# Order of the PSUM banks in the down projections, and the split of the convolution's taps and the turning of the residual in the odd stage

## The reference, cut to what matters

```python
def swiglu(h, w_gu, w_down):
    g, u = jnp.split(h @ w_gu, 2, axis=-1)
    return (jax.nn.silu(g) * u) @ w_down

def _odd_mixer(h, w_in, conv_w, conv_b, ln_g, ln_b, w_out):
    proj = jnp.einsum('bsd,de->bse', h, w_in)
    val, gt, z = three slices of CONV_CHANNELS each
    g = (val * jax.nn.sigmoid(gt)).astype(jnp.float32)
    c = lax.conv_general_dilated(g, kern, window_strides=(1,), padding=[(CONV_KERNEL - 1, 0)],
        dimension_numbers=('NWC', 'WIO', 'NWC'), feature_group_count=CONV_CHANNELS)   # 31 taps a channel
    c = c + conv_b
    mu, var = mean and variance of c over the channels
    c = (c - mu) * lax.rsqrt(var + LN_EPS) * ln_g + ln_b
    y = jax.nn.silu(c) * jax.nn.silu(z)
    return jnp.einsum('bse,ed->bsd', y, w_out)
...
x = x + _odd_mixer(rmsnorm(x), ...)
return _rmsnorm(x, final_norm)
```

## Time and profile before

| what | value |
|---|---|
| time, median of 3 runs | 1538.62 us (1537.76 to 1538.62) |
| span of the profiled execution | 1539.7 us, 1.1 above that median |
| PE busy | 1481.8 us, 96% of the span |
| DVE, ACT, POOL busy | 886.2, 619.4, 381.8 us |
| mean granted clock of TensorE | 0.988 of full speed |
| DMA | 178.45 MB, 116 GB/s over the span |

### The profile page before, as it was taken

How to read it: one execution, slowest core, us unless ns; L and a number is a source line. 1 busy time by engine, 2 the same in 40 slices (tenths; PEclk the granted TensorE clock), 3 DMA queues, 4 the chain that set the end, 5 groups by cost and what they waited for, 6 DMA issues and landing times. The chain is left out here.

```text
span 1539.7 us, 19037 instructions
## 1 busy us (share of the span) xinstructions
PE 1481.8 (96%) x7030; PEld 1168.6 (76%) x7030; DVE 886.2 (58%) x1265; ACT 619.4 (40%) x943; POOL 381.8 (25%) x493
## 2 busy tenths in 40 slices
PE   5999999999999999899999999999999999999998
PEld 3788888888877777458888888888777778777656
DVE  5767425633573566846633434422556556798986
ACT  3432212222443443745542222222531235777755
POOL 3111001000000000013003888520202100599930
PEclk9899999999999999999999999999999999999999
DMA  9887625333244122003433333373124223222211
GB/s 347 279 279 260 203 83 181 107 109 101 59 119 116 55 69 73 8 15 89 130 89 109 123 110 96 112 265 96 55 82 126 81 86 116 75 70 77 75 55 55
DMA packets 203878, 178.45 MB, mean 116 GB/s; under 512 B 7451, under 2 KB 182095, under 8 KB 203286
## 3 DMA queue, kind: packets, MB, share of 16 engines
q1 hardware_dynamic: 187462, 121.87, 26.8%
q0 software_dynamic: 15184, 53.41, 9.9%
q10 hardware_dynamic: 1152, 2.10, 0.4%
HBM read 168.89 MB, written 8.46 MB: 115 GB/s over the span
## 5 line engine op out<-in xcount | busy, mean ns | idle before, releaser
L2053 PE MATMUL ps<-h_hi,w_hi 128*128 128x512 f32 x1176 | 473.4, 403 | 2.7 <-DVE us L1800 1.2
L2055 PE MATMUL ps<-h_hi,w_lo 128*128 128x512 f32 x1176 | 459.0, 390 | 0.0
L2054 PE MATMUL ps<-h_lo,w_hi 128*128 128x512 f32 x1176 | 458.7, 390 | 0.0
L1280 DVE TENSOR_TENSOR w_lo<-w_stage,w_hi 128x1024 fp32r<-128x1024 f32 x225 | 292.1, 1311 | 219.4 <-ACT w_hi L802 216.9
L802 ACT ACTIVATE w_hi<-w_stage 128x1024 fp32r<-128x1024 f32 x225 | 230.8, 1048 | 186.5 <-PE ps L2055 166.8
L2053 PEld LDWEIGHTS ps<-h_hi,w_hi 128*128 128x128 f32 x1176 | 221.2, 188 | 64.4 <-issue 17.2
L2054 PEld LDWEIGHTS ps<-h_lo,w_hi 128*128 128x128 f32 x1176 | 221.4, 188 | 48.7 <-issue 5.0
L2055 PEld LDWEIGHTS ps<-h_hi,w_lo 128*128 128x128 f32 x1176 | 221.0, 188 | 47.1
L2053 PE MATMUL ps<-a_hi,w_hi 128*128 128x512 f32 x480 | 188.3, 392 | 3.7 <-issue 1.8
L2054 PE MATMUL ps<-a_lo,w_hi 128*128 128x512 f32 x480 | 187.4, 390 | 0.0
L2055 PE MATMUL ps<-a_hi,w_lo 128*128 128x512 f32 x480 | 187.3, 390 | 0.0
(11 more groups left out here) (456 smaller groups left out, 1697.8 us busy)
## 6 DMA issues: line engine op xcount, KB each, us to landing
w_stage<-in_w_gu SPq DMA_DIRECT2D x88, 512.0 KB, 4.2
ada_w<-in_w_ada POOLq DMA_DIRECT2D x72, 512.0 KB, 6.3
w_stage<-in_w_down SPq DMA_DIRECT2D x44, 512.0 KB, 3.6
w_stage<-in_w_in SPq DMA_DIRECT2D x24, 512.0 KB, 3.8
w_stage<-in_odd_w_in SPq DMA_DIRECT2D x24, 512.0 KB, 3.7
w_stage<-in_even_w_in SPq DMA_DIRECT2D x16, 512.0 KB, 3.8
w_stage<-in_w_out SPq DMA_DIRECT2D x8, 512.0 KB, 3.7
mats<-mats_d POOLq DMA_DIRECT2D x4, 1024.0 KB, 6.8
```

The costliest lines, as they stand in the source:

```text
L1280: dve.tensor_tensor(w_lo[:, c % RING], w_in[:, c % RING], w_hi[:, c % RING].bitcast(F32), ALU.subtract).then_inc(w_split, 1)
L2053: pe.matmul(bank, w_hi[:, slot, k], rhs_hi, start=start, stop=False, skip_group_check=True)
L2054: pe.matmul(bank, w_hi[:, slot, k], rhs_lo, start=False, stop=False, skip_group_check=True)
L2055: return pe.matmul(bank, w_lo[:, slot, k], rhs_hi, start=False, stop=stop, skip_group_check=True)
```

## The change

It has three parts.

1. In each of the four down projections the step j = 0 goes through the banks in the order 4, 5, 6, 2, 3, 0, 1, 7. The waits are set apart: none of the three is ahead of banks 4 to 6; bank 2 waits for the product of hidden tile 9, bank 0 for that of tile 10, bank 7 (in the first layer) for `mod_ready`. The steps j = 1 to 10 are as they were.
2. In the odd stage POOL takes 12 taps of each of the first six tiles, and DVE 18. The last two tiles are as they were.
3. The residual is turned in two banks: tiles 1, 3 and 5 in bank 6, the others in bank 7; two tiles at a time after n = 2, 4 and 6, tile 6 after n = 8, tile 7 after n = 10. ACT copies them in the step after. The first sum into bank 6 at n = 8 waits for six copies.

```diff
+DOWN_FIRST = [4, 5, 6, 2, 3, 0, 1, 7]
...
-POOL_TAPS = [13] * 6 + [10, 7]
+POOL_TAPS = [12] * 6 + [10, 7]
 DVE_TAPS = [TAPS - 1 - p - q for p, q in zip(POOL_TAPS, PE_TAPS)]
...
+TURNED_AT = {2: [0, 1], 4: [2, 3], 6: [4, 5], 8: [6], 10: [7]}
+TURN_IN_6 = (1, 3, 5)
+
+
+def turn_bank(kt):
+
+    return 6 if kt in TURN_IN_6 else 7
...
-                    if 4 <= n < 4 + KT:
-                        act.wait_ge(x_turned, n - 3)
-                        act.activation(xT[:, n - 4], ps[7][:], ACT.Copy).then_inc(x_back, 1)
+                    for kt in TURNED_AT.get(n - 1, ()):
+                        act.wait_ge(x_turned, kt + 1)
+                        act.activation(xT[:, kt], ps[turn_bank(kt)][:], ACT.Copy).then_inc(x_back, 1)
...
-                    pe.wait_ge(prod_ready, F0 + HALF)
-                    if ada:
-                        pe.wait_ge(mod_ready, [7, 9][half])
                     for j in range(8):
                         pe.wait_ge(w_split, t1 + j + 1)
                         pe.wait_ge(a_ready, F0 + j + 1)
-                        for kt in range(KT):
+                        for kt in DOWN_FIRST if j == 0 else range(KT):
+                            if j == 0 and kt == 2:
+                                pe.wait_ge(prod_ready, F0 + HALF - 1)
+                            if j == 0 and kt == 0:
+                                pe.wait_ge(prod_ready, F0 + HALF)
+                            if j == 0 and kt == KT - 1 and ada:
+                                pe.wait_ge(mod_ready, [7, 9][half])
                             mm = three(ps[kt][:], (t1 + j) % RING, kt, a_hi[:, j * S:(j + 1) * S],
                                        a_lo[:, j * S:(j + 1) * S], j == 0, False)
...
                 def turn_x(kt):
-                    upto(pe, x_back, kt)
+                    upto(pe, x_back, kt - (1 if kt in TURN_IN_6 or kt - 1 in TURN_IN_6 else 0))
                     for st in range(ST):
-                        mm = pe.transpose(ps[7][:, st * P:(st + 1) * P], xT[:, kt, st * P:(st + 1) * P], ident[:])
+                        mm = pe.transpose(ps[turn_bank(kt)][:, st * P:(st + 1) * P], xT[:, kt, st * P:(st + 1) * P], ident[:])
                     mm.then_inc(x_turned, 1)
...
-                    if 3 <= n < 3 + KT:
-                        turn_x(n - 3)
+                    for kt in TURNED_AT.get(n, ()):
+                        turn_x(kt)
                     if n == 8:
+                        pe.wait_ge(x_back, 6)
                         pe.wait_ge(cv_ready, 1)
```

## The result

The changed kernel takes **1523.89 us** (1523.25 to 1524.0, four runs), the kernel before beside it 1538.19 (1535.07 to 1538.62): the ratio is 0.9911, interval 0.9897 to 0.9924, or 14.3 us less. One thing has to be known for this number: the times of the kernel before come in groups (of 76 further executions, which ran beside the experiments, 48 lie at 1535.2 to 1536.9, 25 at 1537.6 to 1539.1 and 3 at 1541.4 to 1541.5, median 1536.2), and three of the first four were of the second group. Against the median of these 76 the change wins 12.2 us (14 executions of it have a median of 1523.97). One more execution of the kernel before took 1869.56 us at a granted clock of 0.748 and is left out of every comparison.

The account below looks back on a forecast made before the run. PE, busy 96% in order, was taken to lose only idle time, with PE, DVE and POOL within 1.5 us at the odd stage's end. Gains 5.5 + 5.8 = 11.3 us from median 1538.6 gave 1527.3, range 1524.7 to 1532.0.

Parts of the forecast that it names:

- the order of the engines: Odd stage's end: POOL ends 8.2 us earlier, DVE 6.6, PE only 4.7, so PE is last.
- The down projections: Four starts of the down projections: PE's pauses go, 5.5 us in all, bounds 3.5 and 5.8.
- So three starts give 1.0 each: Three later down-projection starts: PE's lost time of 1.01 us each goes, 3.0 in all.
- I take the whole 0.92 + 1.54 = 2.5: First down-projection start: PE's 0.92 us wait for bank 7 and 1.54 of half clock behind it both go.
- The odd stage: Fewer POOL taps and two-bank turning: last sum starts 5.8 us earlier, bounds 1.3 and 8.2.
- The edits with no cost: ACT's paired copies and bank 6's wait for six copies at n = 8 were to cost nothing.
- DVE recovering half or none of its waits: Odd stage: 5.3 us of DVE's `w_hi` waits stay, 1531.8, chance 0.15; none recovered, 1537.1, chance 0.05.
- The clock after pairs of transposes: Residual's turning: each of three transpose pairs brings a clock fall of 1.5 us; 1528.2, chance 0.08.
- POOL last: Odd stage's end: PE's part not binding, POOL stays last, stage gains 8.2 us; 1524.9, chance 0.07.
- Down projections gain nothing: Down-projection starts: something else holds j = 0, only the odd stage's 5.8 us gained; 1532.8, chance 0.04.
- POOL's adds lengthened: Odd stage: 40 of POOL's 89 adds take the long form, 162 us instead of 151.6; 1543.5, chance 0.03.
- against the median 1538.6, which lies 1.1 lower: Starting level: the 11.3 us gain subtracted from the kernel before's median 1538.6, not its profiled 1539.7, giving 1527.3.

Follow-up runs that it names:

- pe_taps12: Changed kernel with PE doing 12 instead of 14 taps of the last tile, two going to DVE; 1522.48 us, ratio 0.9903 to the kernel before.
- turn_only: Kernel before with only the residual's turning in two banks, old taps and old down projections; 1536.44 us, ratio 1.0002.
- down_only: Kernel before with only the new bank order and separate waits of the down projections; 1530.03 us, ratio 0.9955.
- pool11: Changed kernel with POOL at 11 and DVE at 19 taps in the six tiles; 1529.24 us, ratio 0.9951 to the kernel before.
- thirds: Changed kernel with DVE's 18 taps of a tile cut 5, 6, 7 instead of 6, 6, 6; 1524.74 us, ratio 0.9917 to the kernel before.
- before_again: The kernel before, unchanged, run again for a second profile; 1536.46 us.
- after_again: The changed kernel, unchanged, run again beside the kernel before; 1524.0 us, ratio 0.9924.
- taps_only: Kernel before with only POOL at 12 and DVE at 18 taps in six tiles; 1532.77 us, ratio 0.998.
- before_third: The kernel before, unchanged, run once more beside mod_first and thirds; 1536.16 us, ratio 0.9997.
- mod_first: Changed kernel with the mod_ready wait put back ahead of the first layer's whole down projection; 1527.08 us, ratio 0.9937 to the kernel before.

## Why the prediction was right, and where it failed

The two mechanisms and the order of the engines were right; the time fell outside the range by the level from which the gain was subtracted, and by 1.6 us in a stretch that no term priced.

**The down projections: right in kind, one term mis-sized.** "So three starts give 1.0 each" measured 1.14 each, as the slow steps behind each pause go with it. "I take the whole 0.92 + 1.54 = 2.5" is the wrong size: 1.04 is certain, and the half clock that I priced as certain came in three of seven profiles. The reason given for it (no pause, no fall) holds in all seven profiles without the pause, which by their number is likely, not shown. Certain sum 4.5 instead of 5.5; nobody was late behind it, as said.

**The odd stage: right, 6.1 for 5.8.** POOL ended 7.8 earlier (8.2 said; its adds of over 2 us are 21 before and after, as assumed), DVE's waits went from 10.6 to 0.7, PE was the last and had its small waits for `w_lo`. What was off inside was the margin. PE was to end 4.7 earlier and ended 5.3 earlier, like the `w_lo` that it needs last; DVE was to end 6.6 earlier and ended 9.1 earlier, so it was 2.98 ahead of PE instead of 0.9. Most of DVE's surplus is that two of its last `w_lo` took 1.22 and 1.21, where they took 2.14 and 2.05 before (the one of the earlier trace rows kept its length, 1.88 and 1.86). Of the `w_lo` beside an add 3 were short before and 9 are now; the prediction took their lengths as given. That surplus was worth nothing, because PE's end counted; and it was the room that pe_taps12 used.

**The edits with no cost** cost nothing: no wait stands at L2541, and none at bank 6.

**The rivals.** DVE recovering half or none of its waits: refuted (0.7 left). The clock after pairs of transposes: refuted here, 1.00 in the window behind the pairs in the changed kernel (and in 1310 to 1322, behind the first), and in turn_only over 1321 to 1352 as well. The rule of the Trainium skill (TensorE: Matmul & The Clock Gate, Part 4: PE-mode transpose) may stand, but 1.04 us of transposes in a full stream did not bring the clock down. POOL last: refuted, PE was, and the stage gave 6.1 and not 8.2; that its 1524.9 lies nearest to the measured time is luck. Down projections gain nothing: refuted by down_only. POOL's adds lengthened: refuted in this change (143.8 for 89 adds, 1.62 each, against 1.60); pool11 and thirds show that the contention behind it is real, and that the instruction that comes second pays for it.

**What put the time 0.8 below the range** is the step "against the median 1538.6, which lies 1.1 lower". I subtracted the gain from a level that was no property of the kernel. Three runs had happened to lie 2.4 above the median of the 76, and the profiled execution higher still, with the clock down behind the first reduction and at the even norm. The "1.1" compares a span with a time, too: in every later run the time is 1.7 above the span of the same execution, so the profiled one with its 1539.7 belongs to the group at 1541.4, and its rows were priced as if they were the usual case. From 1536.2 the same terms would have given 1524.9, against 1523.97 measured. So the 3.4 between 1527.3 and 1523.89 are 2.4 of the level and 1.6 that no term priced (below), less 0.7 by which the terms were too large (11.3 against 10.6). The range was made from the terms' uncertainty alone; that of the level, some 2 us, was not in it.

**What is accounted for, and what stays open.** 4.5 + 6.1 = 10.6 of the 12.2 are in stretches that the change touches. The rest, 1.6, is as much as stands in the attention between them, which took 62.4 in six profiles and 60.8 in seven (64.1 in the first) with the same instructions there; all three profiles of the changed kernel have 60.8, both later ones of the kernel before 62.4. The windows at its end differ by the clock: 0.79 in before_again above, and in after_again

```profile
666.00:674.00 8.00, 6.30 (x43) 4.83 (x44) 2.82 (x9) 4.60 (x11) 0.00 (x0) 1.00 0.00 0
```

But taps_only, with the down projections of before, has 60.8, and down_only, with the new ones, 62.4. So the part changed does not decide it alone. Whether the changed kernel as a whole meets the better case more often (12 of its 14 executions lie in its lowest group, 48 of 76 of the kernel before) is not settled by these numbers. Over all kernels here there is more to say for it: of the 34 executions of kernels without the pause at the first start, 31 lie within 1.9 us of the fastest of their kernel, and of the 114 with it, 69, which chance would hardly give if executions are independent of each other. But the medians of both kernels lie in their lowest groups, so this does not explain the 1.6.

## What to carry to other kernels

Where several engines arrive within a microsecond or two of each other, price the end of each one and ask which is last afterwards; edits that gain 3.4 and 0.0 alone gave 6.1 together, and the idle time that the new profile showed on the engine that was early (2.98) was the next step's room. An idle stretch of PE is worth more than its length where a clock fall can follow, but take as certain only what more than one execution shows. And before a forecast is subtracted from a median, ask how far three runs of one kernel can lie from its usual time, and put that into the range.

## What the runs showed of the hardware that was not expected

The same one-column matmuls and the same 0.9 us of idle were followed by 1.2 GHz in some executions and by 2.4 GHz in others, of one and the same kernel (before, against before_again and before_third). In mod_first the fall came 1.5 us behind the pause (from 173.01 on), after six matmuls at full pace, not with the first one as in the earlier trace rows. And the placement of an instruction by 0.7 us (1336.60 to 1337.28) made it half as long again (1.21 to 1.87): of DVE's `w_lo` and POOL's add, the one that started first kept its length. Behind a `w_lo` that came second the next add was long as well (2.15 for 1.29). So what `w_lo` costs DVE beside POOL is a matter of which of the two comes first, more than of how many there are, while it costs POOL about one long add either way.
